# The first loads of a decoder block: g_norm ahead of x, and x's first slice as two loads of one k-tile each

## What is computed

```
h = rmsnorm(x, g_norm)                      # x * rsqrt(mean(x*x) + eps) * g_norm
z = h @ w_in                                # 2048 x 12296: q, k, v and gates of 16 heads, forget logits, merge gates
oa = diff_attention(...) ; oa = rmsnorm(oa, g_subln) * (1 - lam_init) * silu(ga)
ob = forgetting_attention(...) * silu(gb)
m  = sigmoid(ma) * (oa @ w_proj_a) + sigmoid(mb) * (ob @ w_proj_b)
out = rmsnorm(x + m @ w_out, g_final)
```

## Time and profile before

| | |
|---|---|
| median of 3 runs | 762.3 us (762.3 to 762.76) |
| the profiled execution | 762.72 us, span 760.9 us |
| TensorE busy | 751.2 us, 99% of the span, 3632 matmuls |
| VectorE busy | 422.1 us (55%) |
| ScalarE busy | 365.8 us (48%) |
| GpSimd busy | 76.3 us (10%) |
| DMA | 143.80 MB, mean 189 GB/s |
| chain that ended last | TensorE 96%, issue 1%, DMA 1% |

### The profile page before, as it was taken

The page is one execution under the profiler, slowest core; times in us unless marked ns, Lnnn a source line. Parts: engine busy times, 40 slices in busy tenths (PEclk is TensorE's granted clock), DMA queues, the critical chain, the costliest instruction groups (busy, mean ns, idle before and its releaser), DMA issues.

```text
span 760.9 us, 9586 instructions
## 1 busy us (share of the span) xinstructions
PE 751.2 (99%) x3632; PEld 628.7 (83%) x3632; DVE 422.1 (55%) x616; ACT 365.8 (48%) x556; POOL 76.3 (10%) x153
## 2 busy tenths in 40 slices
PE   8999999999999999999999999999999999999996
PEld 6898888888888888888888888888888888888886
DVE  6754555555555566566665564444445666565552
ACT  6563554445544555445545554443444443444541
POOL 0001111101121221122202000000000000001110
PEclk9999999999999999999999999999999999999999
DMA  8747554554555545554545555555555555855642
GB/s 315 267 159 257 175 185 165 169 191 166 182 174 171 177 166 171 179 178 164 184 166 167 178 173 183 189 192 194 194 194 193 192 180 193 347 193 191 189 145 111
DMA packets 39885, 143.80 MB, mean 189 GB/s; under 512 B 4568, under 2 KB 4576, under 8 KB 39328
## 3 DMA queue, kind: packets, MB, share of 16 engines
q1 hardware_dynamic: 38576, 139.81, 54.8%
q10 hardware_dynamic: 1008, 1.84, 0.7%
q0 software_dynamic: 256, 1.54, 0.5%
HBM read 141.06 MB, written 2.11 MB: 188 GB/s over the span
## 4 chain that ended last, share of the span: by engine, by line
PE 96%; issue 1%; DMA 1%; DVE 0%; ACT 0%; DVEq 0%; POOLq 0%; POOL 0%; ACTq 0%
PE Z L219 29%; PE Z L221 29%; PE Z L220 29%; PE Z L340 3%; PE A L285 1%; PE A L253 1%; PE B L267 1%; PE Dk L276 1%; PE B L264 1%; DMA g_col<-in_g_cols 1%; PE C L294 0%; PE B L302 0%; PE A L302 0%; DVE w_lo L621 0%; ACT w_hi L422 0%
## 5 line engine op out<-in xcount | busy, mean ns | idle before, releaser
L621 DVE TENSOR_TENSOR w_lo<-w_raw,w_hi 128x1024 fp32r<-128x1024 f32 (+1 forms) x252 | 309.6, 1231 | 302.6 <-ACT w_hi L422 300.8
L422 ACT ACTIVATE w_hi<-w_raw 128x1024 fp32r<-128x1024 f32 (+1 forms) x247 | 261.6, 1060 | 348.2 <-PE Z L221 343.1
L219 PE MATMUL Z<-w_hi,hT_hi 128*128 128x512 f32 (+2 forms) x880 | 337.8, 384 | 0.4 <-DVE w_lo L621 0.4
L221 PE MATMUL Z<-w_hi,hT_lo 128*128 128x512 f32 (+2 forms) x880 | 335.3, 381 | 0.0
L220 PE MATMUL Z<-w_lo,hT_hi 128*128 128x512 f32 (+2 forms) x880 | 335.1, 381 | 0.0
L219 PEld LDWEIGHTS Z<-w_hi,hT_hi 128*128 128x128 f32 x880 | 165.4, 188 | 32.0 <-issue 0.6
L221 PEld LDWEIGHTS Z<-w_hi,hT_lo 128*128 128x128 f32 x880 | 165.4, 188 | 31.9
L220 PEld LDWEIGHTS Z<-w_lo,hT_hi 128*128 128x128 f32 x880 | 165.5, 188 | 30.5
L219 PE MATMUL Z<-w_hi,oT_hi 128*128 128x512 f32 x128 | 50.1, 391 | 0.0
L221 PE MATMUL Z<-w_hi,oT_lo 128*128 128x512 f32 x128 | 49.9, 389 | 0.0
L220 PE MATMUL Z<-w_lo,oT_hi 128*128 128x512 f32 x128 | 49.8, 389 | 0.0
(11 more groups left out here) (161 smaller groups left out, 485.2 us busy)
## 6 DMA issues: line engine op xcount, KB each, us to landing
w_raw<-in_w_main SPq DMA_DIRECT2D x251, 512.0 KB, 3.3
w_raw<-in_w_fl SPq DMA_DIRECT2D x4, 528.0 KB, 4.5
x_sb<-in_x SPq DMA_DIRECT2D x1, 2048.0 KB, 9.2
x_sb<-in_xT ACTq DMA_DIRECT2D x4, 256.0 KB, 7.4
x_sb<-in_xT SPq DMA_DIRECT2D x4, 256.0 KB, 5.6
rows<-c_rows_dram POOLq DMA_DIRECT2D x1, 1024.0 KB, 6.2
rows<-in_g_final SPq DMA_DIRECT2D x1, 1024.0 KB, 11.2
out_y<-gates SPq DMA_DIRECT2D x2, 384.0 KB, 2.5
```

Source lines behind the costliest of these rows:

```text
L219: pe.matmul(acc, a_hi, b_hi, start=first, stop=False)
L221: return pe.matmul(acc, a_lo, b_hi, start=False, stop=last)
L422: act.activation(w_hi[:, t % RING, 0:n], w_raw[:, t % RING, 0:n], ACT.Copy).then_inc(hi_ready, 1)
L621: dve.tensor_tensor(w_lo[:, t % RING, 0:n], w_raw[:, t % RING, 0:n], w_hi[:, t % RING, 0:n].bitcast(fp32), ALU.subtract).then_inc(lo_ready, 1)
```

## The change

The load of g_col becomes the first on ScalarE's queue. x slice 0 is loaded by two DMAs of one k-tile each (128 rows of 1024 bytes, where a slice in one load has 128 rows of 2048), each with a semaphore of its own, and `x_part(0)` waits for each k-tile by itself. Slice 3 moves from ScalarE's queue to SP's, ahead of weight tile 3, so that ScalarE still issues five loads.

```
--- before.py
+++ after.py
@@ -143,7 +143,7 @@
         ACT_OUT, DVE_OUT, LAST_OUT = slice(0, 3 * CHUNK // 2), slice(3 * CHUNK // 2, 3 * CHUNK), slice(3 * CHUNK, 4 * CHUNK)
 
         raw_loaded = [sem(f"raw_loaded{i}") for i in range(RING)]
-        first_half = sem("first_half")
+        first_half, x_first = sem("first_half"), sem("x_first")
         hi_ready, lo_ready, w_used = sem("hi_ready"), sem("lo_ready"), sem("w_used")
         evac = [sem("evac0"), sem("evac1")]
         x_loaded = [sem(f"x_loaded{i}") for i in range(TILES)]
@@ -192,7 +192,7 @@
                 sp.dma_start(w_raw[:, t % RING, 0:width(t)], src).then_inc(raw_loaded[t % RING], 16)
 
             for t in range(TILES):
-                if t >= 4:
+                if t >= 3:
                     sp.dma_start(xT_sb[:, 2 * t:2 * t + 2, :], xT[:, 2 * t:2 * t + 2, :]).then_inc(x_loaded[t], 16)
                 if t == 0:
                     sp.dma_start(w_raw[:, 0, 0:CHUNK], w_main[0][:, 0:CHUNK]).then_inc(first_half, 16)
@@ -428,9 +428,12 @@
 
             def x_part(j):
 
-                act.wait_ge(x_loaded[j], 16)
                 for kk in range(2):
                     k = 2 * j + kk
+                    if k == 0:
+                        act.wait_ge(x_first, 16)
+                    elif kk == 0 or j == 0:
+                        act.wait_ge(x_loaded[j], 16)
                     act.activation(hT_hi[:, k, :], xT_sb[:, k, :], ACT.Copy, scale=g_col[:, k:k + 1]).then_inc(xh_ready, 1)
 
             def x_square(j):
@@ -438,9 +441,10 @@
                 act.activation(x_sq[:, 2 * j:2 * j + 2, :], xT_sb[:, 2 * j:2 * j + 2, :], ACT.Square,
                                scale=D_MODEL ** -0.5).then_inc(x_squared, 1)
 
-            act.dma_start(xT_sb[:, 0:2, :], xT[:, 0:2, :]).then_inc(x_loaded[0], 16)
             act.dma_start(g_col[:], g_cols).then_inc(g_loaded, 16)
-            for j in range(1, 4):
+            for k in range(2):
+                act.dma_start(xT_sb[:, k:k + 1, :], xT[:, k:k + 1, :]).then_inc((x_first, x_loaded[0])[k], 16)
+            for j in range(1, 3):
                 act.dma_start(xT_sb[:, 2 * j:2 * j + 2, :], xT[:, 2 * j:2 * j + 2, :]).then_inc(x_loaded[j], 16)
             act.wait_ge(warm_ready, 1)
             act.activation(table_probe[:], warm[:, 0:1], ACT.Copy)
```

## The result

The changed kernel takes 764.97 us, the median of 7 runs (764.08 to 766.2), where the kernel before took 762.3 (762.02 to 763.0) beside it: a ratio of 1.0035, 95% interval 1.0023 to 1.0046. It is 2.7 us slower, outside the range given; the forecast was 762.4. The profiled execution took 765.43 us with a span of 763.6, against 762.72 and 760.9.

The account below looks back on a forecast made before the run. It took the start-up ahead of TensorE's unbroken matmuls as the bound: first matmul 0.57 us earlier, a new 0.77 us gap, tile 1 0.1 us later. That +0.1 on the 762.3 median gave 762.4, range 761.6 to 763.2.

Parts of the forecast that it names:

- the two moments named: At start-up, the first matmul (6.24 us before the change) and the start of tile 1 (11.00) decide the time.
- g_col first: On ScalarE's queue, g_col lands at about 3.65 us instead of 5.64 and nothing waits for it any longer.
- First half: First k-tile of x slice 0: 1.35 us behind g_col, landing at 5.0; first matmul at 5.67, 0.57 us earlier.
- Second half: Second k-tile of x slice 0: 1.75 us for 128 turns, landing at 6.75, between 5.4 and 8.3.
- Second gap: On TensorE, the 0.70 us gap closes and one of 0.77 us opens two matmuls later; third matmul at 7.44.
- Tile 1 by slice 1: Slice 1 lands at 9.05, 0.8 us later, so tile 1 starts at 11.10 against 11.00: 0.1 us lost.
- The clock: On TensorE, a rise at 10.4 us as before recovers half the third matmul's 0.2 us delay; tile 0 ends 0.1 late.
- Slice 3 to SP: Moving slice 3's load to SP's queue ahead of w_raw tile 3 costs nothing; tile 2 has 0.9 us to spare.
- rival three: Slower through the second gap; strong form has slice 0's second half at 8.3, tile 1 at 12.95, 764.3; chance 0.13, strong 0.04.
- the mild form: Rival three with loads as forecast but the clock rising at 11.6, 4.2 us after the last gap: 0.7 lost, 763.0.
- Rival one: Loads cost their bytes, turns are free: first matmul at 5.53, no second gap, tile 1 at 10.62, 761.9; chance 0.22.
- Rival two: With the gap closed, TensorE's clock reaches 2.4 GHz before 10.4 us; tile 1 at 10.32, 761.6; chance 0.08.

Follow-up runs that it names:

- the gap filled: Changed kernel plus two products of zeros on TensorE between the second and third matmul, loads untouched: 763.81 us, ratio 1.0021.

## Why the prediction was wrong

**What bounds the kernel** was right: the whole difference is made ahead of tile 2, and the two moments named decide it.

**g_col first**: right. It lands at 3.55 against 3.65 and nothing that TensorE needs waits for it. "VectorE's casts can go at 4.34": they go at 3.61, hidden.

**First half**: 5.2 against 5.0, first matmul 5.80 against 5.67. Right, and a little late; the middle of 0.89 and 2.0 is 1.45 and not the 1.35 that was added, and with it the forecast would have been 5.1.

**Second half: the step that failed.** The term was 128 turns of 1024 bytes at 1.75 us, "the middle, as the size stands in the middle" between g_col's 64-byte rows and slice 0's of 2048. It measured 8.07 - 5.2 = 2.9 us, and 8.07 is near the upper bound of 8.3. The interpolation was over the wrong size: 128 rows cost nearly the same whether they hold 1024 or 2048 bytes (2.9 us here, 2.63 for slice 1 in the kernel before). The run with the halves ahead of g_col paid 1.6 us for 128 rows of 64 bytes beside 3.9 KB rows, the price of the earlier trace rows being 0.89 beside 2.3 KB; what is beside a turn sets the price more than its own size. The second half has both: 128 turns with 4096 + 1024 bytes are 0.66 MB, about 1.8 us at the 352 to 397 GB/s of the last two windows of the earlier trace rows. That is the forecast's figure: its 1.75 agreed with the bytes by luck, not by its argument. For the missing 1.1 us the rate is the likeliest cause, though no run shows it alone: 185, 249 and 332 GB/s in the three microseconds from 4 to 7, where before had 383 and 384 in the first two. The 0.8 us of missing bytes (above) would cover most of it. Nothing in the trace of before pointed to that fall.

**Second gap**: the place was right (two matmuls later), the size was not, 2.12 us against 0.77.

**Tile 1 by slice 1**: forecast 9.05, measured 9.95; 1.9 us behind the second half where 2.3 was taken, so all of the lateness is the second half's. w_hi is ready at 11.85, so the loads alone would let tile 1 start at 11.91, 0.9 us late.

**The clock: the second step that failed.** "If the clock rises at 10.4 as before, half of that is recovered." It was at 2.4 GHz already during the first two matmuls, fell in the gap, and made all ten others of tile 0 and the first three of tile 1 slow. In the profiled execution that is 13.08 - 11.91 = 1.17 us ahead of tile 1 and 16.48 - 13.08 - 2.76 = 0.64 us in it; with the 0.9 of the loads this is the 2.7. The medians give the clock less, 1.0 to 1.2, as its moment differs between executions: the mean granted clock of the seven runs of the changed kernel goes from 0.992, in its two slowest (765.43 and 766.2), to 0.999.

**Slice 3 to SP** at nothing: right, by the run that took it back.

**The rivals.** What came is rival three in its strong form, on the mechanism given: "if the second half costs what 2048 byte rows cost (8.3), the third matmul is at 9.0", priced 764.3 and given 0.04. It measured 8.07 and 8.65; the point from which it decides, about 6.6, was passed by 1.5 us. Its argument against, "bytes in front of slice 1 are the same", did not hold: slice 1, the fourth load and no longer the third, landed at 9.95. That the price of 764.3 came near the 764.97 is in part luck. It had slice 1 at 10.9 and 1.95 us lost by the loads alone; they lost 0.9 in the profiled execution, and the rest came through the clock, which was put only into the mild form, as a later rise. That the clock could fall once more was in no case. The prediction's own sign of being wrong, tile 1 later than 12, came with 13.08. Rival one was refuted for two loads (8.07), though a single load of the same rows behaves as it says (5.4). Rival two's early rise did occur, and the gap undid it. The range left out an end that it had itself worked out: the upper bound of the turn's price and the loss of the clock are not independent, as the same late load makes both.

**Open**: why a third load lands with the other queue's third even when it has 64 rows, as in the split by partitions; why the second half hardly moved from 4.5 to 5.25 us; and why both queues slow down to 150 to 290 GB/s from 4 to 5 us when g_col is first on ScalarE's queue.

## What to carry to other kernels

Two queues that take turns make a small load cost what stands beside it: before a load is split, count the loads and rows of everything ahead of the wait, and set beside each the other queue's load of the same number. Splitting a critical load into two puts every load behind it one place further back; rows of half the size in one load cost nothing. Idle time of TensorE among its first matmuls can take the clock with it, and then costs twice. It can do so ahead of the first of them as well as behind, so a gap is worth looking for in its new place when a change moves it.

## What the hardware showed that was not expected

- **The clock falls again after short gaps, but not after each.** It fell in the changed kernel in a gap of 2.12 us behind two matmuls. In the run with all but the split it fell 0.85 us after a gap of 1.89 us, while matmuls ran. In the run with slice 0 in one load of 256 rows it fell just behind a gap of 1.69 us that had twelve fast matmuls ahead of it (four of tile 1 then took 1.66 us), while in the run that held tile 1 back for slice 0 a gap of 1.60 us left it up. The matmuls of the run with 256 rows:

```profile
8.09 1.19 PE L340 MATMUL Z<-w_lo,hT_hi 128*128 128x512 f32 x4
...
10.97 1.86 PE L340 MATMUL Z<-w_hi,hT_hi 128*128 128x512 f32 x4 [1.69 <-ACT w_hi L422]
...
12.63 1.91 PE L340 MATMUL Z<-w_hi,hT_lo 128*128 128x512 f32 x4
```

- **What the clock grants differs between executions** of one kernel. The changed kernel's mean granted clock was 0.992 to 0.999 in its seven runs, which spread over 2.1 us, and 0.997 to 0.999 in the eleven with the gap filled, which spread over 0.6 (763.49 to 764.08). The Trainium skill, page 'TensorE: Matmul & The Clock Gate', Part 1, has the moment at which the clock rises vary from run to run. The profiles agree: the products of zeros took 3.61 us where it rose during them and 4.21 where it did not.
- **The rate of the first loads depends on what is first.** With g_col ahead on ScalarE's queue, 4:5 us had 156 to 286 GB/s in every run whose tile 1 loads were not held back; with slice 0 ahead of g_col on it 350 to 393. In the run that held tile 1 for g_col it was 193 GB/s though ScalarE's queue moved all the packets of that microsecond.
- **A load issued earlier came later.** Tile 1's weights, issued at 3.57 beside the slices, landed at 9.8; issued at 5.43, behind them, at 9.2.
